# A two-layer DeltaNet and pooling step: second chunk solved as U(v - KS), outer products spread over the stage, GpSimd takes first fades and first operand halves

## The reference, cut to what matters

```python
m = jnp.where(strict, bc[..., :, None] * kk * decay, 0.0)
a_mat = m + jnp.eye(CHUNK, dtype=m.dtype)
rhs = jnp.concatenate([vc * bc[..., None], kc * (bc * jnp.exp(G))[..., None]], axis=-1)
sol = lax.linalg.triangular_solve(a_mat, rhs, left_side=True, lower=True, unit_diagonal=True)
w_val, k_cd = sol[..., :dv], sol[..., dv:]
...
    u = w_n - jnp.einsum('bhck,bhkv->bhcv', kcd_n, s)
    o = jnp.einsum('bhck,bhkv->bhcv', qd_n, s) + jnp.einsum('bhij,bhjv->bhiv', qk_n, u)
    s = s * cd_n[..., None, None] + jnp.einsum('bhck,bhcv->bhkv', kt_n, u)
...
o = o * lax.rsqrt(jnp.mean(o * o, axis=-1, keepdims=True) + EPS) * o_norm.astype(jnp.float32)
o = o * jax.nn.silu(z.reshape(bsz, t, DN_HEADS, DN_DV).astype(jnp.float32))
```

## Time and profile before

| | |
|---|---|
| median of three runs | 1521.64 us |
| profiled execution | 1525.01 us, its span 1523.4 us |
| PE busy | 1488.2 us, 98% of the span |
| DVE, ACT, POOL busy | 530.9, 361.9, 94.2 us |
| layer A's solve and what follows up to a_out | about 204 to 298 us of the span |
| experts | from 644 us on |

### The profile page before, as it was taken

The page is one execution under the profiler, slowest core; times in us unless marked ns, Lnnn a source line. Parts: engine busy times, 40 slices in busy tenths (PEclk is TensorE's granted clock), DMA queues, the critical chain, the costliest instruction groups (busy, mean ns, idle before and its releaser), DMA issues.

```text
span 1523.4 us, 33315 instructions
## 1 busy us (share of the span) xinstructions
PE 1488.2 (98%) x14679; PEld 868.3 (57%) x14679; DVE 530.9 (35%) x877; ACT 361.9 (24%) x633; POOL 94.2 (6%) x168
## 2 busy tenths in 40 slices
PE   9999988799999999999999999999999999999998
PEld 8989877699999999733333333333333333333332
DVE  6767854566665576501101101101101101111113
ACT  6566565454444442400000000000000000000001
POOL 0011135000000000020000000000000000000010
PEclk9999998799999999999999999999999999999999
DMA  6778631355554585999999999999999999999993
GB/s 261 295 270 283 222 129 46 148 196 191 171 183 164 194 331 207 366 396 419 418 402 420 419 400 420 403 415 420 402 419 419 401 418 420 397 419 419 418 419 145
DMA packets 78054, 490.71 MB, mean 322 GB/s; under 512 B 9304, under 2 KB 9560, under 8 KB 53216
## 3 DMA queue, kind: packets, MB, share of 16 engines
q1 hardware_dynamic: 70000, 460.41, 76.2%
q0 software_dynamic: 7920, 28.25, 5.3%
HBM read 464.71 MB, written 23.92 MB: 321 GB/s over the span
## 4 chain that ended last, share of the span: by engine, by line
PE 90%; DVE 5%; ACT 3%; DMA 1%; issue 1%; SPq 0%; DVEq 0%; ACTq 0%
PE PP L2618 38%; PE PP L1958 24%; PE PP L2628 19%; DVE dlo L396 2%; ACT dhi L390 1%; DMA ring<-in_mkv 1%; PE PP L2284 1%; PE PP L2183 1%; PE PP L2076 1%; PE PP L2060 0%; PE PP L2501 0%; PE PP L2052 0%; PE PP L2038 0%; DVE ring L1332 0%; PE PP L2319 0%
## 5 line engine op out<-in xcount | busy, mean ns | idle before, releaser
L2618 PE MATMUL PP<-ring,gen 128*32 128x448 f32 x6144 | 578.8, 539 | 1.2 <-DVE gen L1812 1.2
L2618 PEld LDWEIGHTS PP<-ring,gen 128*32 128x32 f32 x6144 | 199.9, 110 | 379.2 <-issue 377.5
L2628 PE MATMUL PP<-ring,gen 128*32 128x512 f32 x2688 | 289.9, 592 | 0.0
L1958 PE MATMUL PP<-uh,dhi 128*128 128x264 f32 x736 | 213.4, 290 | 2.8 <-DVE dlo L396 1.9
L1958 PE MATMUL PP<-ul,dhi 128*128 128x264 f32 x736 | 208.9, 284 | 0.0
L1958 PE MATMUL PP<-uh,dlo 128*128 128x264 f32 x736 | 208.8, 284 | 0.0
L396 DVE TENSOR_TENSOR dlo<-ring,dhi 128x2048 fp32r<-128x2048 f32 (+2 forms) x85 | 175.5, 2065 | 93.3 <-ACT dhi L390 93.2
L1135 ACT ACTIVATE ubuf<-PP 128x448 f32<-128x448 f32 x48 | 22.6, 544 | 780.2 <-PE PP L2618 780.2
L1896 DVE TENSOR_TENSOR gen<-ubuf,PP 128x448 f32<-128x448 f32 x48 | 26.9, 616 | 517.6 <-PE PP L2618 517.6
L2628 PEld LDWEIGHTS PP<-ring,gen 128*32 128x32 f32 x2688 | 87.4, 110 | 199.7 <-issue 199.7
L390 ACT ACTIVATE dhi<-ring 128x2048 fp32r<-128x2048 f32 (+2 forms) x85 | 147.0, 1730 | 111.5 <-PE PP L1958 91.3
(11 more groups left out here) (491 smaller groups left out, 1363.7 us busy)
## 6 DMA issues: line engine op xcount, KB each, us to landing
ring<-in_w_up SPq DMA_DIRECT2D x256, 896.0 KB, 20.7
ring<-in_w_down SPq DMA_DIRECT2D x112, 1024.0 KB, 21.1
ring<-in_wi SPq DMA_DIRECT2D x22, 1024.0 KB, 4.9
ring<-in_a_in SPq DMA_DIRECT2D x18, 1024.0 KB, 6.9
ring<-in_wo SPq DMA_DIRECT2D x16, 704.0 KB, 4.1
slot_rows<-ring POOLq DMA_DIRECT2D x25, 384.0 KB, 4.5
ring<-in_mkv SPq DMA_DIRECT2D x8, 1024.0 KB, 4.9
ring<-in_kc SPq DMA_DIRECT2D x8, 1024.0 KB, 9.2
```

The source lines that it names most:

```text
L1958: mm = pe.matmul(out, lhs[l], rhs[r], start=first and i == 0, stop=last and i == 2)
L2618: mm = pe.matmul(bank((c // KD % 2) * SG + g)[SL * q:SL * (q + 1), 0:FQ], xs[:, at_:at_ + SL], w[:, q * FQ:(q + 1) * FQ], start=(k == 0), ...
L2628: return pe.matmul(out[SL * quarter:SL * (quarter + 1), :], hT[:, at_:at_ + SL], w[:, k * D + h * 512:k * D + (h + 1) * 512], start=(j == ...
```

## The change

- **Second chunk.** PE multiplies the decayed keys `kd` with S into PP[1] (after.py line 2417), DVE subtracts that from `vtok[1]` in place (1585), and PE multiplies U1 with the difference (2423). K U1, its negated copy WT and the pair of accumulated products go. `kd` is made by POOL (635) as keys times exp(G), next to `qd` (636); ACT's eight scaled copies into `kdec` go.
- **Order on PE.** `outer(3)`, `outer(4)` and `head_sums(0)` stand ahead of U1's product; `outer(5)` and the spread of chunk 0 ahead of the second output; `head_sums(1)` between `outer(6)` and `outer(7)`; the attention blocks of a_out tile 0 ahead of chunk 1's spread and of the second state. In the solve `pair_z(0)`, `half_y(0)` and `half_z(0)` move ahead of chunk 1's steps.
- **Outputs.** ACT squares from PSUM (1016) with no copy into `cat`; `gated` on DVE reads PSUM (1561); the 8 sample columns are squared and gated apart (1028, 1567).
- **Fading.** POOL takes groups 0, 1, 4, 6, 7 and ACT groups 2, 3, 5. POOL's group 0 stands inside the solve, around `diagonal(3, 1)`.
- **First operands.** The low half of the attention blocks of `cat` (673) and that of a_out 0 (398) are subtracted by POOL, between its state stores; DVE's `dense_low` of a_out 0 goes.
- **Elsewhere.** `ublk` 2 and 3 lie in another place, the second state goes to PP[3], the roots to banks 4 and 3, chunk 1's spread to PP[1] and PP[2].

The core of the diff:

```diff
+FADED_EARLY = [0, 1, 4, 6, 7]
+FADED_ACT = [2, 3, 5]
...
@@ gpsimd
+            diagonal(1, 1)
+            pool.wait_ge(s("dl_ud"), 4)
+            pool.wait_ge(s("dl_dt"), 2 * H + 1)
+            pool.wait_ge(s("l2_done"), 2 * H)
+            pool.tensor_tensor(heads128(kd), act[:, H:2 * H, P:SEQ], heads128(qd), ALU.mult).then_inc(s("dl_ud"), 1)
+            pool.tensor_tensor(heads128(qd), act[:, 0:H, P:SEQ], heads128(qd), ALU.mult).then_inc(s("dl_ud"), 1)
+            pool.wait_ge(s("dl_ud"), 6)
+            diagonal(2, 0)
+            diagonal(2, 1)
+            diagonal(3, 0)
+            pool.wait_ge(s("dl_ud"), 9)
+            pool.wait_ge(s("sd_mm"), 1)
+            faded(0, (0,))
+            pool.wait_ge(s("faded_late"), 1)
+            diagonal(3, 1)
+            pool.wait_ge(s("dl_ud"), 10)
+            faded(0, (1,))
...
-            pool.wait_ge(s("sd_in"), 6)
-            for k in range(FADES, 8):
-                faded(k)
-            for i in range(4):
+
+            def sent(i):
                 pool.wait_ge(s("state_new"), 4 * (i + 1))
                 pool.dma_start(outs["state"][i], state[:, i * DCH:(i + 1) * DCH]).then_inc(s(f"state_stored{i // 2}"), 16)
+
+            faded(1)
+            faded(4)
+            sent(0)
+            faded(6)
+            sent(1)
+            faded(7)
+            pool.wait_ge(s("m_hi"), 3 * KD + 2)
...
+            pool.tensor_tensor(lo[:, H:H + XH, :], cat[:, H:H + XH, :], hi[:, H:H + XH, :].bitcast(F32), ALU.subtract).then_inc(s("m_lo"), 1)
+            sent(2)
+            dense_low(pool, AT["a_out", 0])
+            sent(3)
@@ scalar
-                    for x in range(H):
-                        ins_ = a.activation(kdec[:, x * P:(x + 1) * P], PP[0][:, x * P:(x + 1) * P], ACT.Copy, scale=ceG[:, H + x:H + x + 1])
...
-                a.activation(sqv[:, :, parts[c]], cat[:, 0:H, parts[c]], ACT.Square).then_inc(s("on_sq"), 1)
+                a.wait_ge(s("dl_o"), c + 1)
+                a.activation(sqv[:, :, c * P:(c + 1) * P], heads128(PP[2 * c][:, :]), ACT.Square).then_inc(s("on_sq"), 1)
...
+            faded(2)
             solved(0)
-            faded(2)
-            a.wait_ge(s("dl_tok"), 5)
-            for g in range(2):
-                a.activation(half(WT, g), bank(g), ACT.Copy, scale=-1.0).then_inc(s("dl_u"), 1)
             faded(3)
             a.wait_ge(s("dl_o"), 1)
-            a.activation(cat[:, 0:H, parts[0]], PP[0][:, :].rearrange("p (m c) -> p m c", m=H), ACT.Copy).then_inc(s("dl_cat"), 1)
...
+            a.activation(sqv[:, :, SEQ:T], cat[:, 0:H, SEQ:T], ACT.Square).then_inc(s("on_sq"), 1)
             squares(0)
+            faded(5, (0,))
+            head_root(0)
             solved(1)
...
+            faded(5, (1,))
             a.wait_ge(s("att_cat"), 2)
-            a.wait_ge(s("sd_outer"), 16)
             a.activation(cat_h[:, H:H + XH, :], cat[:, H:H + XH, :], ACT.Copy).then_inc(s("m_hi"), 1)
+            a.wait_ge(s("state_stored0"), 32)
+            dense_high(a, AT["a_out", 0])
@@ vector
             v.tensor_copy(Sb, PP[2][:, :]).then_inc(s("S_done"), 1)
             state_sum(3)
+            v.wait_ge(s("dl_tok"), 5)
+            v.tensor_tensor(vtok[1], vtok[1], PP[1][:, :], ALU.subtract).then_inc(s("dl_vt"), 1)
+            state_sum(4)
+            sample_gated()
             gated(0)
-            state_sum(4)
             head_inverse(0)
+            state_sum(5)
             v.wait_ge(s("on_mm"), 2)
...
             state_sum(6)
             gated(1)
+            head_inverse(1)
             state_sum(7)
-            cat_low(H, H + XH, slice(0, T))
-            head_inverse(1)
...
-            dense_low(v, AT["a_out", 0])
@@ tensor
-            for x in range(H):
-                mm = pe.matmul(PP[0][:, head(x)], kdec[:, head(x)], Ub[1][:, head(x)], start=True, stop=True)
-            mm.then_inc(s("dl_tok"), 1)
...
+            outer(3)
             pe.wait_ge(s("S_done"), 1)
+            pe.wait_ge(s("dl_un"), 4)
             for x in range(H):
-                pe.matmul(PP[1][:, head(x)], Ub[1][:, head(x)], vtok[1][:, head(x)], start=True, stop=False)
-                mm = pe.matmul(PP[1][:, head(x)], WT[:, head(x)], Sb[:, head(x)], start=False, stop=True)
+                mm = pe.matmul(PP[1][:, head(x)], kd[:, head(x)], Sb[:, head(x)], start=True, stop=True)
+            mm.then_inc(s("dl_tok"), 1)
+            outer(4)
+            head_sums(0, bank(4), 0, P)
+            pe.wait_ge(s("dl_vt"), 3)
+            for x in range(H):
+                mm = pe.matmul(PP[1][:, head(x)], Ub[1][:, head(x)], vtok[1][:, head(x)], start=True, stop=True)
...
             pe.wait_ge(s("on_done"), 1)
+            a_out_tile(0, 0, XH, lambda i: base_a + 1)
             pe.wait_ge(s("head_inv"), 3)
...
+            pe.wait_ge(s("state_new"), 16)
             for x in range(H):
+                mm = pe.matmul(PP[3][:, head(x)], ktail[1][:, head(x)], wrow[1][:, head(x)], start=True, stop=True)
+            mm.then_inc(s("dl_ds"), 1)
+            a_out_tile(0, XH, len(order), lambda i: base_a + need[XH + i]).then_inc(s("aout_mm"), 1)
```

More of the change, by code:

```diff
@@ L283, in build @@
         urow = cut(gen, DS + 576, 128)
-        ublk = [cut(gen, DS + 704 + 512 * i, 512) for i in range(2)] + [cut(ring, arena + 2112 + 512 * i, 512) for i in range(2)]
+        ublk = [cut(gen, DS + 704 + 512 * i, 512) for i in range(2)] + [cut(ring, arena + CT * PRE + 2 * H * ACTW + 512 * i, 512) for i in range(2)]
         sil = [cut(gen, SC + 2640 + 264 * i, 264) for i in range(2)]
@@ L582, in _, with faded @@
             store(outs["conv"], convio)
-            def faded(k):
-                for g in groups(k):
+            def faded(k, parts=(0, 1)):
+                for i in parts:
+                    g = groups(k)[i]
                     for q in range(4):
@@ L630, in _ @@
             diagonal(1, 0)
[L631 removed]
+            pool.wait_ge(s("dl_ud"), 3)
             sample_blocks()
@@ L634, in _ @@
             diagonal(1, 1)
-            for lv in range(2, LV - 1):
-                for c in range(2):
-                    diagonal(lv, c)
+            pool.wait_ge(s("dl_ud"), 4)
[14 more added lines that the diff above has]
+            faded(0, (1,))
+            pool.wait_ge(s("faded_late"), 2)
             for c in range(2):
@@ L945, in _ @@
             turned(3, 0)
-            faded(0, (0,))
             diagonal(3, 1)
@@ L2416, in _, with a_out_tile @@
             mm.then_inc(s("on_mm"), 1)
-            outer(5)
             for x in range(H):
-                mm = pe.matmul(PP[1][:, head(x)], ktail[1][:, head(x)], wrow[1][:, head(x)], start=True, stop=True)
-            mm.then_inc(s("dl_ds"), 1)
+                pe.wait_ge(s("dl_u"), 2 + x // 4 + 1)
+                pe.matmul(PP[2][:, head(x)], Sb[:, head(x)], qd[:, head(x)], start=True, stop=False)
+                mm = pe.matmul(PP[2][:, head(x)], wrow[1][:, head(x)], PT[1][:, x, :], start=False, stop=True)
+            mm.then_inc(s("dl_o"), 1)
             outer(6)
+            head_sums(1, bank(3), P, T - P)
             outer(7)
+            order = [(k, k) for k in (*range(H, H + XH), *range(H))]
+            base_a = 3 * KD + 1
+            need = [1] * XH + [3] * 4 + [4] * 4
+            def a_out_tile(t, k0, k1, ready=None):
+                return tile(bank(AOUT_BANK[t])[:, 0:T], weights(AT["a_out", t], 12), 0, (cath[0], catl[0]), T, order[k0:k1],
+                            first=k0 == 0, last=k1 == len(order), ready=ready)
             pe.wait_ge(s("on_done"), 1)
-            head_sums(1, bank(0), P, T - P)
+            a_out_tile(0, 0, XH, lambda i: base_a + 1)
             pe.wait_ge(s("head_inv"), 3)
             pe.wait_ge(s("dl_cat"), 2)
-            pe.wait_ge(s("state_new"), 16)
             for x in range(H):
                 at_, r = 32 * (x % 4), x // 4
-                mm = pe.matmul(bank(4 + x % 4)[:, r * (T - P):(r + 1) * (T - P)],
+                mm = pe.matmul(bank(2 + x % 4)[:, r * (T - P):(r + 1) * (T - P)],
                                ident[at_:at_ + 32, at_ + r:at_ + r + 1].to_broadcast([32, P]),
@@ L2433, in _ @@
             mm.then_inc(s("on_mm"), 1)
-            order = [(k, k) for k in (*range(H, H + XH), *range(H))]
-            base_a = 3 * KD + 1
-            need = [1] * XH + [3] * 4 + [4] * 4
-            for t in range(KD):
-                w = weights(AT["a_out", t], 12)
-                if t == 0:
-                    pe.wait_ge(s("on_done"), 1)
-                if t == 1:
-                    pe.wait_ge(s("head_rt"), 3)
-                if t == 2:
+            pe.wait_ge(s("state_new"), 16)
+            for x in range(H):
+                mm = pe.matmul(PP[3][:, head(x)], ktail[1][:, head(x)], wrow[1][:, head(x)], start=True, stop=True)
+            mm.then_inc(s("dl_ds"), 1)
+            a_out_tile(0, XH, len(order), lambda i: base_a + need[XH + i]).then_inc(s("aout_mm"), 1)
+            for t in range(1, KD):
+                if t == 6:
```

(3 more changed lines are left out.)

104 lines of the change are left out of this document (43 added, 61 removed).

## The result

| | before | changed |
|---|---|---|
| median | 1520.99 us (4 runs) | 1505.53 us (4 runs, 1503.13 to 1506.19) |
| ratio to before | | 0.9891 [0.9865, 0.9917] |
| profiled execution, its span | 1525.01, 1523.4 us | 1505.22, 1503.6 us |
| mean granted clock of the profiled execution | 0.987 | 0.999 |

What follows compares the result with a forecast made beforehand. PE's stream was taken as the bound: tile 1 of a_out from 304.6 to 290.5, 14.1 us, less 0.6 contention, 13.5, less 1.5 for the clock, 12.0. From the median 1521.64 to 1509.6 us, range 1506.5 to 1516.5.

Steps and rivals of the forecast that it cites:

- The clock I leave as it is, back at 255.7: Inside the solve: PE's half clock from 242.0 stays until 255.7 us, so nothing is gained there.
- The bound that I set for it, 1.7: Solve: gain of 1.7 us if full clock came back before chunk 1's Gram product, 3.71 at half, about 1.8 at full.
- Between 0 and 2.6 I take 1.5: End of the stage into a_out: a low-clock stretch could lie on tile 1; 1.5 us taken off the gain.
- Contention, 0.6: Solve: POOL's four group 0 fades slow DVE's short sample-row steps near 230 us; 0.6 us lost, between 0 and 2.4.
- an estimate of 1.2: Solve: by the skill's SBUF exclusion rule three DVE steps each wait out part of a fade, 1.2 us instead of 0.6.
- For some 0.4 us: Solve, at 242: a 64x64 product put ahead of 32x32 ones on PE starts the Gram product at 251.1, not 251.53.
- PE behind U0 v0: PE from 256.9: K U1's 1.98 gone, subtraction hidden, spread at 271.0; gate of chunk 1 at 278.3 instead of 288.45.
- DVE's end chain: DVE from chunk 1's gate to a_out 1's low half: 12.1 us instead of 14.4, two low halves going to POOL.
- 2.45 and 3.57: POOL's subtractions for the low halves of attention and a_out 0: 2.45 and 3.57 us, done at 278.8, needed at 279.4.

Runs made afterwards that it cites:

- e5: Changed kernel with the low halves of the attention blocks and of a_out 0 back on DVE instead of POOL; ratio to before 0.9932.
- e6: Changed kernel with outer(3) and outer(4) behind U1's product, outer(5) behind the second output, DVE's sums likewise; ratio to before 0.9958.
- e12: Kernel before, unedited, profiled again; 66.6 us from the first Gram product to tile 1 of a_out.
- e2: Changed kernel, unedited, timed and profiled again; ratio to before 0.9898.
- e1: Kernel before, unedited, timed and profiled again; ratio to before 1.0003.
- e11: Kernel before, unedited, profiled again; 62.5 us from the first Gram product to tile 1 of a_out.
- e16: Changed kernel, unedited, profiled a third time; 47.9 us from the first Gram product to tile 1 of a_out.
- e13: Changed kernel with the eight products of K S issued twice, 1.8 us more PE work; ratio to before 0.9906.
- e3: Changed kernel with the orders inside the solve on PE, ACT and DVE put back as before; ratio to before 0.9914.
- e4: Kernel before with only the solve's orders on PE and ACT as in the changed kernel; ratio to before 0.9988.
- e10: Kernel before with useless products, two each, ahead of both spreads and a_out, where PE waits for DVE; ratio to before 1.0009.
- e9: Kernel before with four useless 128x512 products behind the first Gram product; ratio to before 1.0027.
- e8: Changed kernel with the second state's decay moved from DVE to POOL, behind its low half of a_out 0; ratio to before 0.9894.

## Why the forecast gain was too small

Most of the mechanism was right: the time is PE's stream until a_out, and behind U0 v0 the steps came within 0.6 us of their forecast. The clock ahead of it was wrong. Point by point:

- **The failed step: "The clock I leave as it is, back at 255.7".** I took the half clock of 242 to 255.7 for a property of the PE order, to stay. The changed kernel has full clock there in all three profiles, and before has the long stretch in two of six. The bound that I set for it, 1.7, was for the Gram product alone, though the same row has PE busy 13.70 of 13.70 us at half clock, so up to half of that stood to be won; the interval turned out 5.7 shorter, 5.2 of it the stretch. The forecast for the profiled execution, 1513.0, is 7.8 above the measured 1505.22. From the median, 1509.6 is only 4.1 above 1505.53, and that is luck: the profile was one of the long executions, 3.4 above the median, and its excess covered nearly half of the miss.
- **"Between 0 and 2.6 I take 1.5"** for a low stretch at the end: it was 0 in every profile of the changed kernel. That this is because PE is filled where it had waited is what e5 and e6 point to.
- **Contention, 0.6.** One of DVE's three short steps took longer beside the fades, in each of the three profiles 0.38 or 0.39 instead of 0.23:

```profile
229.59 0.23 DVE L1496 TENSOR_TENSOR gen<-gen 128x64 f32<-128x64 f32 x1
229.85 0.38 DVE L1497 TENSOR_TENSOR gen<-gen,small 128x64 f32<-128x64 f32 x1
```

  So the fades cost 0.15. The Trainium skill's rule (page "SBUF — State Buffer", Who interferes with whom), by which I had an estimate of 1.2 for three such steps, isn't borne out for all: 1496 has two SBUF operands too, ran inside the same run of four fades (229.19 to 231.58) and was not longer. But I had looked at the fades alone. The two products that make `kd` and `qd` also stand inside the solve now, and a copy of DVE that takes 0.29 in each profile of before took 0.90, 1.45 and 1.71 in the three of the changed kernel. In each it ended some 0.16 us after POOL's second product (222.84 here), whenever it had begun:

```profile
220.45 2.39 POOL L636 TENSOR_TENSOR gen<-ring,gen 128x1024 f32<-128x1024 f32 x1
222.10 0.90 DVE L1443 COPY gen<-gen 32x256 f32<-32x256 f32 x1
```

  Little of that reaches PE. From the first such copy of the solve (207.44 here) to the Gram product the changed kernel takes 28.2 to 28.6 us; in the kernel before it is 27.9 in e12, which like the first profile and e2 has no half clock on the way, and 28.1 and 28.3 in e1 and e11, which like e16 have 3.4 us of it early. The whole term is some 0.2 to 0.7.
- **PE behind U0 v0**: K U1 gone, subtraction hidden by `outer(4)`, 1.222 against my 1.225: right (15.7 against 16.2; e13 shows the price). The interval to the gate of chunk 1 was 0.6 longer than forecast: the spread took 2.02 and not 1.79, and DVE's sums of `outer(6)` ended 1.2 behind it and not 0.8.
- **DVE's end chain** 12.1: 11.9. **POOL** 2.45 and 3.57: 2.45 and 3.46, so the second subtraction ended at 272.2, with room:

```profile
265.75 2.45 POOL L673 TENSOR_TENSOR catl<-gen,cath 128x1056 fp32r<-128x1056 f32 x1 [1.56 <-ACT cath L1035]
...
268.78 3.46 POOL L398 TENSOR_TENSOR dlo<-ring,dhi 128x1536 fp32r<-128x1536 f32 x1
```

- **"For some 0.4 us", inside the solve**: 0.45, but for ACT's fades and not for the trade of places on PE (e3, e4): a right number for a wrong reason.
- **What reaches the end.** From the first product behind the norm to the end of the span before took 1174.9 us and the changed kernel 1175.7 in the first profiles, and within each group of runs the difference is 0.8 to 1.3. So about 1 us of the gain is given back in the later stages. I had not priced that, and why it is so stays open.

The account against the mean of the six profiles of before, 64.9 us from the Gram product to tile 1: less 47.9 is 17.0. Of these, 2.2 are ahead of U0 v0 (forecast 0.2: 0.45 is the wait for ACT, the rest the long stretch, met in two of six), and 14.8 behind it (13.9 forecast, against a profile without the short stretch). Less about 1 for the later stages, some 16 us, where the timings say 15.5 and, in another group, 0.9898 or 15.6. What stays open is what brings the long stretch: with the old order of the solve on PE it came in three of ten profiles (before, e1, e10), with the new one in none of eight, which may be chance.

## What to carry to other kernels

Profile the kernel before several times before pricing a clock stretch: what returns in each execution belongs to the kernel and goes with its cause, what comes in some of them has to be averaged, and a gain worked out on one profile is to be taken from that one's own time. Before leaving a low stretch in the sum, look whether PE is full in it: then up to half of its length can come back. Fill a wait with work that has to be done anyway; useless products won nothing here. The price of an order is not the sum of its waits: in e3, e5 and e6 half clock came back with them. For the whole change the waits are 7.0 us fewer, and by the slope the clock is worth about as much again.

## What the runs showed of the hardware that was not expected

- The same program at the same step (second chunk's solve) ran PE at half clock for 13.7 us in some executions and not in others. The Trainium skill (page "TensorE: Matmul & The Clock Gate", What's actually happening) says of the start of a kernel that the monitor's window is free-running and that the count of slow matmuls varies from run to run. These profiles show such a variation in the middle of a kernel, 18.0 and 12.8 us for the same interval; that it has the same cause isn't shown.
- PE was busy 5.70 of 5.70 us, with the Gram product and then products of 32x32 and one `outer`, before the clock fell at 240.9 in e1:

```profile
235.20:240.90 5.70, 5.70 (x155) 4.74 (x152) 3.00 (x6) 2.45 (x8) 4.41 (x6) 1.00 0.01 3
```

  A PE that is always busy is no sign of full clock. In e11 it ran the same products and the clock stayed.
- A float32 product with 512 columns is two records. Over 128 rows a record took 0.43 us back to back at full clock (e9, 3.44 for eight), over 32 rows, as in `outer`, 0.265 (1.06 for four).
- A 32x256 copy of DVE that began during a 128x1024 product of POOL ended some 0.16 us after it, five times out of five (e2, e6, e8, e16 and the first profile, 0.90 to 1.71 us instead of 0.29), while DVE's 128x64 steps beside the fades lost 0.15 us or nothing.
- POOL's low half of 128x1536 took 3.46 us against DVE's 1.76, and that of 128x1056 2.45 against 1.25.
